# A two-layer decoder trunk: the undilated values are turned by VectorE and DMA, and statistics change row order by VectorE copies instead of fold matmuls

## The chip, the cores and the metric

The kernel runs on one core of a Trainium2 chip. The metric is the device time of one execution in microseconds, the median of three runs. Everything is float32; a product is made of three matmuls of rounded parts (high by high, low by high, high by low).

## The reference

The program computes a two-layer causal decoder for 512 tokens of width 1024. Layer 0 mixes tokens by a mixture of three dilated window attentions, layer 1 by differential attention; after each mixer come a squared-ReLU MLP and a gated input embedding. Only layer 0's mixer is touched by the change. Cut to what matters:

```python
# h: (1, 512, 1024); 16 heads of 64; groups (window, dilation) = (128,1), (512,4), (2048,16)
qkv = (h @ w_qkv).reshape(B, T, 3, 3, 16, 64)
for g in range(3):
    # query t attends to t, t-d, ..., t-window, with a bias by distance
    logits = q @ k.T * 64**-0.5 + bias ; lse = logsumexp(logits)
    out[g] = exp(logits - lse) @ v
alpha = softmax(stack(lse), axis=0)      # weight of each group, per position and head
o = sum(alpha * out) @ w_o
```

## The kernel before, in words

Tokens are in two row orders. The projections have them by residue mod 4 (all tokens with t mod 4 = 0, then 1, and so on): group 1 (dilation 4) has its rows in that order, and group 2 (dilation 16) uses the same tiles with a mask. The undilated group 0 needs its rows by position. So the statistics of group 0 (minimum and sum per row, `near_stat`) and those of groups 1 and 2 (`far_stat`) belong to differently ordered rows, and to merge the softmaxes they must be carried from one order to the other and back (`near_share`).

The first mixer runs in nine steps (`a_steps`): step s projects for pair s of heads and attends for pair s-1. Step 0 only projects, step 8 (the drain) only attends. Each step has nine slots; slot i has one projection unit of 24 matmuls of 512 columns on the tensor engine. In odd steps the first four slots are one large product for the values of groups 1 and 2 in four token tiles (`values_unit`, slots 0 to 3), evacuated by VectorE in slot 3 (L1423). The values of group 0 are projected in slot 0 of even and slot 4 of odd steps, and turned one slot later (`A_TURN_V`).

All orders are written out by hand. Each engine walks the slots, and within a slot the statements of its own `sub_a`:

- VectorE: masked logits and minimum (slots 0 and 1), the low part of the next unit's weights (`next_lo`, L1236), the merge of the statistics (slot 2), scaling of the four groups of probabilities (`scale_a`, L1324; slots 2, 3, 4, 5), a turn of each within 32x32 blocks (L1350; `blocks`), and at the slot's end the evacuation of the unit (L1436, L1423).
- GpSimd: when a group's blocks are ready, 16 DMAs put the blocks in their places (L902), 64 a step. Blocks and DMAs together transpose the probabilities.
- Tensor engine: scores (slots 0 and 1), the first fold in slot 2 (L1892), the second in slot 4 (L1901), the turn of the values in slot 1 or 5 (L1778), and at the end of slot 8 the value products of the four groups in the order 2, 3, 0, 1 (L1850), each of which waits until its 16 DMAs have landed.

A fold carries statistics between the row orders. VectorE spreads them against a pattern (`quarter`, L1356 and L1391), four small matmuls with `fold` sum rows 32 apart, and VectorE copies the result back from PSUM (L1365, L1397).

A unit waits for the evacuation of the units before it (L1716):

```python
wait(te, evac_done, u - (3 if is_first_up(u) else 2 if is_third(u) else 1))
```

For unit 4 of an odd step this means that the first three of the four evacuations (L1423) of the values' product are through.

Of the kernel before, what the change touches and what calls it, by code (L numbers as in the profile page):

```python
# [35 lines left out]
ALU = mybir.AluOpType  # L36
ACT = mybir.ActivationFunctionType

P = 128
# [3 lines left out]
NT = T // P  # L43
# [33 lines left out]
DRAIN_SPREAD, DRAIN_MERGE, DRAIN_NEAR = 3, 4, 6  # L77
# [171 lines left out]
def build(nc, x, p, rel_bias, a_w_qkv, a_w_o, b_w_qkv, b_w_o, lq1, lk1, lq2, lk2, subln, norm_mix,  # L249
          norm_mlp, w_ff1, w_ff2, norm_ple, w_gate, w_proj, final_norm, selector, out):  # L250
    ctx = ExitStack()
    with ctx:
# [61 lines left out]
        fold = sb("fold", [P, SUB])  # L314
        quarter = sb("quarter", [P, NT])
# [11 lines left out]
        spread_stat = merge[:, 0:64].rearrange("p (a r) -> p a r", r=NT)  # L327
        spread_share = merge[:, 64:96].rearrange("p (a b) -> p a b", b=NT)
# [29 lines left out]
        far_in = logits[:, 0:4 * NT]  # L358
# [43 lines left out]
        def near_in(has_proj):  # L402

            return (turned if has_proj else attn)[:, 0:2 * NT]

# [20 lines left out]
        def merge_slots(has_proj):  # L426

            return (A_SPREAD, A_MERGE, A_NEAR) if has_proj else (DRAIN_SPREAD, DRAIN_MERGE, DRAIN_NEAR)
# [133 lines left out]
        quarter_ready = sem("quarter_ready")  # L562
        fold_ready = sem("fold_ready")
# [29 lines left out]
        qk_ready = sem("qk_ready")  # L593
        vt_ps = sem("vt_ps")
# [6 lines left out]
        spread_stat_ready = sem("spread_stat_ready")  # L601
        far_ps = sem("far_ps")
# [3 lines left out]
        spread_share_ready = sem("spread_share_ready")  # L606
        near_ps = sem("near_ps")
# [245 lines left out]
        def _(pool):  # L853
# [7 lines left out]
            pool.memset(quarter[:, :], 0.0).then_inc(quarter_ready, 1)  # L861
            pool.wait_ge(quarter_ready, 1)
            for r in range(NT):
                pool.memset(quarter[r * SUB:(r + 1) * SUB, r:r + 1], 1.0).then_inc(quarter_ready, 1)
            pool.wait_ge(const_ready, 5)
            pool.wait_ge(quarter_ready, 1 + NT)
            pool.tensor_tensor(fold[:, :], ident[:, 0:SUB], ident[:, SUB:2 * SUB], ALU.add
                               ).then_inc(fold_ready, 1)
            for r in range(2, NT):
                pool.wait_ge(fold_ready, r - 1)  # L870
                pool.tensor_tensor(fold[:, :], fold[:, :], ident[:, r * SUB:(r + 1) * SUB], ALU.add
                                   ).then_inc(fold_ready, 1)

            pool.wait_ge(fold_ready, NT - 1)
# [23 lines left out]
            for n in range(A_ITEMS * (A_PAIRS - 1)):  # L898
                ph = A_TURN_ORDER[n % A_ITEMS]
                pool.wait_ge(blocks_ready, n + 1)  # L900
                for i, j in itertools.product(range(NT), range(NT)):
                    pool.dma_start(turned_order(probs[ph][j * SUB:(j + 1) * SUB, :])[:, i, :],  # L902
                                   turned_order(blocks[i * SUB:(i + 1) * SUB, ph, :])[:, j, :]
                                   ).then_inc(probs_landed[ph], 16)
# [10 lines left out]
        def _(sc):  # L915
# [96 lines left out]
            def sub_a(s, par, i, has_proj, has_attn):  # L1012
# [16 lines left out]
                _, merge_at, _ = merge_slots(has_proj)  # L1029
# [14 lines left out]
                if has_proj and i == A_TURN_V[par]:  # L1044

                    wait(sc, vt_ps, s + 1)
                    sc.activation(a_buf(par, 0, V), misc[:, :], ACT.Copy).then_inc(v_ready, 1)
# [90 lines left out]
            def sub_b(s, par, i, has_proj, has_scores, has_prev, has_norm):  # L1138
# [22 lines left out]
                if has_scores and i == 0:  # L1161
                    wait(sc, vt_ps, s + A_PAIRS)
                    sc.activation(b_buf(1 - par, V), misc[:, :], ACT.Copy).then_inc(v_ready, 1)
# [65 lines left out]
        def _(ve):  # L1229
# [63 lines left out]
            def start_statistics():  # L1293

                ve.wait_ge(quarter_ready, 1 + NT)
# [30 lines left out]

            def merged(s, n):
# [843 lines left out]
```

## Time and profile before

| | |
|---|---|
| time, median of 3 runs | 1594.29 us (1594.04 to 1595.57) |
| time of the profiled execution | 1594.29 us |
| its span | 1592.4 us |
| tensor engine busy | 1576.4 us, 99% |
| VectorE busy | 919.3 us, 58% |
| ScalarE busy | 590.9 us, 37% |
| GpSimd busy | 286.4 us, 18% |
| tensor engine's granted clock | 0.998 of 2.4 GHz |

The span is what lies between the first and the last instruction of the profiled execution; the time has about 2 us around it. Matmuls overlap: the busy time of one (0.39 us for 512 columns) is longer than the distance to the next start, so costs are read from starts. The steps of the first mixer are at about 68 to 124 us (step 1), then some 58 us each: step 4, an even one, is at 241 to 299 us, step 5, an odd one, at 299 to 357 us.

### The profile page before, as it was taken

To read this page: it belongs to the slowest core of one execution; us is meant where nothing else is said; L and a number is where in the kernel's file an instruction comes from. 1 tells how busy PE (TensorE), PEld (TensorE's weight loads), DVE (VectorE), ACT (ScalarE), POOL (GpSimd) and SP (SyncE) were. 2 spreads that over 40 slices of the span, in tenths; PEclk is the share of its full clock that TensorE was granted. 3 is DMA by queue.
4 is the path that set the end of the run, shared out by engine and by line. 5 is a ranking of instruction groups with operands and counts; after the bars stand their busy time and mean duration, and the time that the engine had idled before them with its cause. 6 is when DMAs were issued, how large, how long until landed. Compare 5 with 4: busy or idle time off the path is not lost.

```text
span 1592.4 us, 22054 instructions
## 1 busy us (share of the span) xinstructions
PE 1576.4 (99%) x8034; PEld 1296.5 (81%) x8034; DVE 919.3 (58%) x1585; ACT 590.9 (37%) x1064; POOL 286.4 (18%) x516
## 2 busy tenths in 40 slices
PE   9999999999999999999999999999999999999998
PEld 7888888888888788888888878888878888888886
DVE  5466466457456844536355766777685363545565
ACT  5324314324324522213123446676552131222344
POOL 2072473474470200000001110000020000000111
PEclk9999999999999999999999999999999999999999
DMA  6565464465443233333333332332233333333341
GB/s 166 151 166 145 141 171 129 140 166 133 120 126 112 79 104 88 100 92 97 100 92 99 99 118 69 106 92 72 73 93 98 90 104 94 92 103 92 93 116 70
DMA packets 314909, 174.84 MB, mean 110 GB/s; under 512 B 38713, under 2 KB 302450, under 8 KB 314850
## 3 DMA queue, kind: packets, MB, share of 16 engines
q1 hardware_dynamic: 300112, 158.61, 35.5%
q0 software_dynamic: 14480, 15.42, 3.5%
q8 instruction: 36, 0.59, 0.2%
q14 instruction: 23, 0.19, 0.0%
q10 hardware_dynamic: 258, 0.04, 0.0%
HBM read 157.11 MB, written 10.60 MB: 105 GB/s over the span
## 4 chain that ended last, share of the span: by engine, by line
PE 89%; POOL 5%; DMA 2%; DVE 1%; ACT 1%; SPq 1%; issue 0%; POOLq 0%; ACTq 0%; DVEq 0%
PE unit_out L1702 24%; PE unit_out L1704 24%; PE unit_out L1703 24%; POOL probs L902 4%; POOL sumsq L910 1%; PE attn L1850 1%; DMA w_raw<-in_a_w_qkv_dram 1%; PE attn L2098 1%; PE turned L1778 1%; PE unit_out L1869 1%; PE unit_out L1870 1%; PE unit_out L1871 1%; PE logits L1702 1%; PE misc L1778 1%; PE misc L1702 1%; PE misc L1704 1%
## 5 line engine op out<-in xcount | busy, mean ns | idle before, releaser
L1702 PE MATMUL unit_out<-act_hi,w_hi 128*128 128x512 f32 x1849 | 725.9, 393 | 1.6 <-DVE act_lo L1251 1.1
L1704 PE MATMUL unit_out<-act_hi,w_lo 128*128 128x512 f32 x1849 | 718.6, 389 | 0.0
L1703 PE MATMUL unit_out<-act_lo,w_hi 128*128 128x512 f32 x1849 | 718.0, 388 | 0.0
L928 ACT ACTIVATE w_hi<-w_raw 128x1024 fp32r<-128x1024 f32 (+3 forms) x256 | 270.9, 1058 | 464.2 <-PE unit_out L1704 368.3
L1702 PEld LDWEIGHTS unit_out<-act_hi,w_hi 128*128 128x128 f32 x1849 | 347.1, 188 | 77.3 <-DVE w_lo L1236 3.0
L1704 PEld LDWEIGHTS unit_out<-act_hi,w_lo 128*128 128x128 f32 x1849 | 347.1, 188 | 72.6
L1703 PEld LDWEIGHTS unit_out<-act_lo,w_hi 128*128 128x128 f32 x1849 | 347.4, 188 | 69.4 <-issue 0.2
L1236 DVE TENSOR_TENSOR w_lo<-w_raw,w_hi 128x1024 fp32r<-128x1024 f32 (+3 forms) x256 | 319.5, 1248 | 102.0 <-ACT w_hi L928 102.0
L902 POOL DMA_DIRECT2D probs<-blocks x448 | 220.3, 501 | 229.7 <-DVE blocks L1350 201.0
L910 POOL TENSOR_TENSOR sumsq<-sumsq,square 128x512 f32<-128x512 f32 x41 | 57.8, 1410 | 1053.6 <-ACT square L956 1051.8
L1098 ACT ACTIVATE act_hi<-hidden 128x512 fp32r<-128x512 f32 x64 | 40.5, 633 | 243.4 <-DVE hidden L1500 243.4
L1497 DVE TENSOR_TENSOR scaled<-unit_out,rstd 128x512 f32<-128x512 f32 x62 | 42.8, 690 | 67.8 <-PE unit_out L1704 67.7
L1315 DVE TENSOR_TENSOR h_a<-h_a,unit_out 128x512 f32<-128x512 f32 x39 | 26.8, 687 | 90.0 <-PE unit_out L1704 90.0
L1315 DVE TENSOR_TENSOR heads<-heads,unit_out 128x512 f32<-128x512 f32 x40 | 27.5, 686 | 84.2 <-PE unit_out L1704 84.2
L1037 ACT ACTIVATE probs<-probs,w_raw 128x256 f32<-128x256 f32 (+1 forms) x128 | 61.7, 484 | 28.2 <-DVE w_raw L1340 28.2
L1503 DVE TENSOR_TENSOR act_lo<-hidden,act_hi 128x512 fp32r<-128x512 f32 x64 | 44.3, 692 | 44.7 <-ACT act_hi L1098 44.7
L1500 DVE SCALAR_TENSOR_TENSOR hidden<-scaled 128x512 f32<-128x512 f32 x64 | 44.3, 692 | 2.2
L1581 DVE CUSTOM_DVE_ANT_0 probs<-logits,bias 128x512 f32<-128x512 f32 (+3 forms) x64 | 28.2, 487 | 26.0 <-PE logits L1704 26.0
L1154 ACT ACTIVATE probs<-probs,low 128x512 f32<-128x512 f32 (+3 forms) x64 | 35.4, 554 | 7.5 <-DVE low L1581 7.5
L1413 DVE TENSOR_TENSOR act_lo<-attn,act_hi 128x512 f32 (+1 forms) x8 | 5.5, 690 | 52.1 <-ACT act_hi L1051 52.1
L943 ACT ACTIVATE act_hi<-heads,gains 128x512 fp32r<-128x512 f32 x24 | 17.3, 722 | 49.1 <-DVE heads L1315 25.6
L1324 DVE TENSOR_SCALAR probs<-probs,w_raw 128x256 f32<-128x256 f32 (+1 forms) x128 | 35.4, 341 | 0.3
(296 smaller groups left out, 1384.2 us busy)
## 6 DMA issues: line engine op xcount, KB each, us to landing
w_raw<-in_w_ff_dram SPq DMA_DIRECT2D x128, 512.0 KB, 4.0
w_raw<-in_a_w_qkv_dram SPq DMA_DIRECT2D x56, 512.0 KB, 4.3
probs<-blocks POOLq DMA_DIRECT2D x448, 32.0 KB, 2.5
w_raw<-in_b_w_qkv_dram SPq DMA_DIRECT2D x24, 512.0 KB, 5.0
w_raw<-in_a_w_qkv_dram SPq DMA_DIRECT2D x32, 256.0 KB, 3.1
w_raw<-in_w_ple_gate_dram SPq DMA_DIRECT2D x16, 512.0 KB, 3.9
bias_tiles_b<-bias_vectors SPq DMA_DIRECT2D x16, 256.0 KB, 4.4
bias<-bias_tiles_b SPq DMA_DIRECT2D x8, 512.0 KB, 3.8
```

The lines of the kernel that those rows point to most:

```text
L902: pool.dma_start(turned_order(probs[ph][j * SUB:(j + 1) * SUB, :])[:, i, :], turned_order(blocks[i * SUB:(i + 1) * SUB, ph, :])[:, j, :]). ...
L910: pool.tensor_tensor(sumsq[:, :], sumsq[:, :], square[n % 2][:, :], ALU.add).then_inc(sumsq_done, 1)
L928: sc.activation(weights_of(u)[0][:, 0:width, :], w_raw[par][:, 0:width, :], ACT.Copy).then_inc(hi_done, 1)
L1037: e = sc.activation(probs[ph][:, cols], probs[ph][:, cols], ACT.Exp, bias=low_col, scale=-1.0, accum_out=sum_col)
L1236: ve.tensor_tensor(lo[:, 0:width, :], w_raw[par][:, 0:width, :], hi[:, 0:width, :], ALU.subtract).then_inc(lo_done, 1)
L1315: ve.tensor_tensor(h[:, n, :], h[:, n, :], unit_out[u.const % 2][:, :], ALU.add).then_inc(evac_done, 1)
L1497: ve.tensor_tensor(scaled[:, :], bank_of(u)[:, :], rstd[:, :], ALU.mult).then_inc(evac_done, 1)
L1500: ve.scalar_tensor_tensor(hidden[:, :], scaled[:, :], 0.0, scaled[:, :], ALU.max, ALU.mult).then_inc(hid_ready, 1)
L1503: ve.tensor_tensor(MID[layer][1][:, n, :], hidden[:, :], MID[layer][0][:, n, :], ALU.subtract).then_inc(hid_done, 1)
L1702: te.matmul(bank, w_k[0], hi, start=start, stop=False)
L1703: te.matmul(bank, w_k[0], lo, start=False, stop=False)
L1704: return te.matmul(bank, w_k[1], hi, start=False, stop=stop)
```

## The change

Four things are edited, all in the first mixer.

1. The four matmuls per pair that turn group 0's values, and ScalarE's copy of the result, are gone. VectorE turns them within 32x32 blocks into `probs_t`, and GpSimd puts the blocks in place by 16 DMAs per pair on a semaphore of their own. In even steps these DMAs stand ahead of the probabilities' 64 in GpSimd's order, in odd steps behind them. VectorE waits for the landing of the previous pair's values before it writes `probs_t` again.
2. Both folds are gone, with `quarter`, `fold` and the spreading. Instead 16 copies of 32 rows each carry the statistics, first from `near_stat` to `far_stat` (slot 2), later from `share` to `near_share` (slot 4).
3. The blocks of each group of probabilities are turned in the slot of their scaling, right behind it, and ahead of the slot's evacuation; before, one slot later and behind the evacuation.
4. The tensor engine waits for the values' landing before the third of its value products. In layer 1 only the counts of the semaphore `v_ready` change.

```diff
-A_SPREAD, A_MERGE, A_NEAR = 1, 2, 4
+A_MERGE, A_NEAR = 2, 4
 A_SCALES = {2: (2,), 3: (3,), 4: (0,), 5: (1,)}
+A_BLOCKS = A_SCALES
-A_BLOCKS = {3: (2,), 4: (3,), 5: (0,), 6: (1,)}
...
 # GpSimd
+            def spread_values(pair):
+
+                pool.wait_ge(values_blocks, pair + 1)
+                to = a_buf(pair % 2, 0, V).rearrange("p (a i q) -> p a i q", a=NT, i=NT)
+                for i, j in itertools.product(range(NT), range(NT)):
+                    pool.dma_start(to[j * SUB:(j + 1) * SUB, :, i, :],
+                                   probs_t[i * SUB:(i + 1) * SUB, j * P:(j + 1) * P].rearrange(
+                                       "p (a q) -> p a q", a=NT)).then_inc(values_landed, 16)
+
+            for step in range(A_PAIRS):
+                if step % 2 == 0:
+                    spread_values(step)
+                for n, ph in enumerate(A_TURN_ORDER) if step else ():
+                    pool.wait_ge(blocks_ready, A_ITEMS * (step - 1) + n + 1)
+                    spread(probs[ph], blocks[:, ph, :], probs_landed[ph])
+                if step % 2:
+                    spread_values(step)
...
 # VectorE, slot 2
-                    wait(ve, far_ps, s)
-                    ve.tensor_copy(far_stat[:, :, 0, :], far_in[:, :].rearrange(
-                        "p (a b) -> p a b", a=2)).then_inc(merge_step, 1)
+                    wait(ve, exp_done, (s - 1).times(A_ITEMS) + 2)
+                    far, near = (x.rearrange("p a (j b) -> p a j b", b=NT) for x in
+                                 (far_stat[:, :, 0, :], near_stat[:, :, :]))
+                    for b, r in itertools.product(range(NT), range(NT)):
+                        last = ve.tensor_copy(far[rows_of(b), :, :, r], near[rows_of(r), :, :, b])
+                    last.then_inc(merge_step, 1)
...
 # VectorE, slot 4
-                    wait(ve, near_ps, s)
-                    ve.tensor_copy(near_share[:, :], near_in(has_proj)).then_inc(near_share_ready, 1)
+                    near, far = (x.rearrange("p (j b) -> p j b", b=NT) for x in (near_share[:, :], share[:, 0, :]))
+                    for b, r in itertools.product(range(NT), range(NT)):
+                        last = ve.tensor_copy(near[rows_of(r), :, b], far[rows_of(b), :, r])
+                    last.then_inc(near_share_ready, 1)
                     wait(ve, near_share_ready, s)
                 if has_attn:
                     for ph in scales_at(has_proj, i):
                         scale_a(s, ph)
+                    for ph in blocks_at(has_proj, i):
+                        wait(ve, probs_ready, (s - 1).times(A_ITEMS) + (A_TURN_ORDER.index(ph) + 1))
+                        to_blocks(blocks[:, ph, :], probs[ph][:, :]).then_inc(blocks_ready, 1)
+                if has_proj and i == A_TURN_V[par]:
+                    wait(ve, evac_done, u)
+                    wait(ve, values_landed, s.times(16 * NT * NT))
+                    to_blocks(probs_t[:, :], a_v_t(i - 1)).then_inc(values_blocks, 1)
...
 # tensor engine
-                if has_proj and i == A_TURN_V[par]:
-                    wait(te, evac_done, u)
-                    wait(te, v_ready, s)
-                    turn(misc, [(a * P, a_v_t(i - 1)[:, a * P:(a + 1) * P])
-                                for a in range(NT)]).then_inc(vt_ps, 1)
                 if has_attn and i == A_UNITS - 1:
                     for n, ph in enumerate(A_TURN_ORDER):
+                        if ph == 0:
+                            wait(te, values_landed, s.times(16 * NT * NT))
                         if has_proj:
                             wait(te, probs_landed[ph], s.times(16 * NT * NT))
```

How this moves instructions is shown at three places. First VectorE in an odd step, from the turn of the first block to the end of slot 3 (before: one row further); `heads` are the four evacuations of the values' product, `blocks` the turned probabilities. Before:

```order
L1350 STREAM_TRANSPOSE blocks<-probs 128x8x4x32
L196 REGISTER_ALU
L1236 TENSOR_TENSOR w_lo<-w_raw,w_hi 128x1024
L1324 TENSOR_SCALAR probs<-probs,w_raw 128x256 x4
L196 ISA
L1423 TENSOR_SCALAR heads<-unit_out,start_scale 128x2x2x128
L196 REGISTER_ALU
L1423 TENSOR_SCALAR heads<-misc,start_scale 128x2x2x128
L196 REGISTER_ALU
L1423 TENSOR_SCALAR heads<-unit_out,start_scale 128x2x2x128
L1423 TENSOR_SCALAR heads<-attn,start_scale 128x2x2x128
L1350 STREAM_TRANSPOSE blocks<-probs 128x8x4x32
```

After:

```order
L1319 STREAM_TRANSPOSE blocks<-probs 128x8x4x32
L196 REGISTER_ALU
L1227 TENSOR_TENSOR w_lo<-w_raw,w_hi 128x1024
L1314 TENSOR_SCALAR probs<-probs,w_raw 128x256 x4
L1319 STREAM_TRANSPOSE blocks<-probs 128x8x4x32
L196 ISA
L1412 TENSOR_SCALAR heads<-unit_out,start_scale 128x2x2x128
L196 REGISTER_ALU
L1412 TENSOR_SCALAR heads<-misc,start_scale 128x2x2x128
L196 REGISTER_ALU
L1412 TENSOR_SCALAR heads<-unit_out,start_scale 128x2x2x128
L1412 TENSOR_SCALAR heads<-attn,start_scale 128x2x2x128
```

The turn of the second block, which stood after the fourth evacuation in slot 4, now stands ahead of the first one in slot 3.

Second VectorE in an even step, from the weight split of slot 1 to the end of the merge's first part in slot 2. Before:

```order
L1236 TENSOR_TENSOR w_lo<-w_raw,w_hi 128x1024
L1436 TENSOR_TENSOR hidden<-unit_out,rstd_q 128x4x4x32
L196 REGISTER_ALU
L1365 COPY w_raw<-logits 128x2x8
L196 REGISTER_ALU
L1368 TENSOR_TENSOR w_raw<-w_raw 128x8
L196 REGISTER_ALU
L1372 TENSOR_TENSOR w_raw<-w_raw 128x16
L196 REGISTER_ALU
L1236 TENSOR_TENSOR w_lo<-w_raw,w_hi 128x1024
```

After:

```order
L1227 TENSOR_TENSOR w_lo<-w_raw,w_hi 128x1024
L196 REGISTER_ALU
L1319 STREAM_TRANSPOSE probs_t<-scaled 128x4x4x32
L1425 TENSOR_TENSOR hidden<-unit_out,rstd_q 128x4x4x32
L1349 COPY w_raw<-w_raw 32x2x2 x16
L196 REGISTER_ALU
L1352 TENSOR_TENSOR w_raw<-w_raw 128x8
L196 REGISTER_ALU
L1356 TENSOR_TENSOR w_raw<-w_raw 128x16
L196 REGISTER_ALU
L1227 TENSOR_TENSOR w_lo<-w_raw,w_hi 128x1024
```

The turn of the values (`probs_t<-scaled`) is added in slot 1, and 16 copies of 32 rows stand where one copy from PSUM stood.

Third GpSimd's whole list of DMAs. Before:

```order
L892 CAST table<-probs 32x16
L895 DMA qk_hi<-selector_dram 96x1824
L896 DMA qk_hi<-selector_dram 1x16x114
L902 DMA probs<-blocks 32x256 x448
L910 TENSOR_TENSOR sumsq<-sumsq,square 128x512 x41
```

After:

```order
L873 DMA qk_hi<-selector_dram 96x1824
L874 DMA qk_hi<-selector_dram 1x16x114
L888 DMA heads<-probs_t 32x4x32 x16
L879 DMA probs<-blocks 32x256 x64
L888 DMA heads<-probs_t 32x4x32 x32
L879 DMA probs<-blocks 32x256 x128
L888 DMA heads<-probs_t 32x4x32 x32
L879 DMA probs<-blocks 32x256 x128
L888 DMA heads<-probs_t 32x4x32 x32
L879 DMA probs<-blocks 32x256 x128
L888 DMA heads<-probs_t 32x4x32 x16
```

The 16 DMAs of the first pair's values come first. Where x32 stands, 16 belong to the values of an odd step, behind its probabilities, and 16 to the next even step, ahead of its probabilities. The probabilities' transfers (32 rows of 256 elements) are 448 as before; the values' have 32 rows of 4 pieces of 32 elements.

## Rows read from the trace of the kernel before

**Rows 1.** The page's first part: busy us, share of the span, instructions.

```profile
PE 1576.4 (99%) x8034; PEld 1296.5 (81%) x8034; DVE 919.3 (58%) x1585; ACT 590.9 (37%) x1064; POOL 286.4 (18%) x516
```

**Rows 2.** PE's waits, 60 to 540 us: us in total, times, longest.

```profile
PE attn L1850 <- DMA probs<-blocks: 1.4, 2, 1.0
```

**Rows 3.** Timeline of PE, step 5 (odd): start us, us, engine, what.

```profile
325.23 0.39 PE L1871 MATMUL attn<-w_hi,act_lo 128*128 128x512 f32 x1
325.55 0.25 PE L1901 MATMUL turned<-w_raw,fold 128*32 128x8 f32 x8
...
327.67 0.39 PE L1704 MATMUL unit_out<-act_hi,w_lo 128*128 128x512 f32 x1
...
336.51 0.39 PE L1704 MATMUL unit_out<-act_hi,w_lo 128*128 128x512 f32 x1
336.75 0.60 PE L1778 MATMUL misc<-ident,scaled 128*128 128x128 f32 x4
...
339.95 0.39 PE L1702 MATMUL unit_out<-act_hi,w_hi 128*128 128x512 f32 x1
```

**Rows 4.** Timeline of PE, step 4 (even).

```profile
255.53 0.39 PE L1704 MATMUL unit_out<-act_hi,w_lo 128*128 128x512 f32 x1
255.77 0.60 PE L1778 MATMUL misc<-ident,scaled 128*128 128x128 f32 x4
256.29 0.26 PE L1892 MATMUL logits<-w_raw,fold 128*32 128x16 f32 x8
...
259.58 0.39 PE L1703 MATMUL unit_out<-act_lo,w_hi 128*128 128x512 f32 x1
```

**Rows 5.** Timeline of DVE, step 5, slot 3 and the start of slot 4.

```profile
322.45 1.15 DVE L1324 TENSOR_SCALAR probs<-probs,w_raw 128x256 f32<-128x256 f32 x4
323.53 0.74 DVE L1423 TENSOR_SCALAR heads<-unit_out,start_scale 128x512 f32<-128x512 f32 x1
...
324.85 0.73 DVE L1423 TENSOR_SCALAR heads<-unit_out,start_scale 128x512 f32<-128x512 f32 x1
...
326.33 1.23 DVE L1350 STREAM_TRANSPOSE blocks<-probs 128x1024 f32<-128x1024 f32 x1
```

**Rows 6.** Timeline of POOL, steps 4 and 5; in brackets the idle time before.

```profile
264.41 7.97 POOL L902 DMA_DIRECT2D probs<-blocks  x16 [27.07 <-DVE blocks L1350]
273.34 23.57 POOL L902 DMA_DIRECT2D probs<-blocks  x48 [0.97 <-issue]
...
337.07 15.62 POOL L902 DMA_DIRECT2D probs<-blocks  x32 [0.99 <-issue]
```

**Rows 7.** Line L902 alone: durations in ns, min/median/max.

```profile
L902 POOL DMA_DIRECT2D probs<-blocks x448: 496/496/631, 87.3 to 466.7; - x150
...
DMA to landing us min/median/max: 1.6/2.5/5.3
```

**Rows 8.** POOL's instructions on the tile qk_hi, the same columns.

```profile
L895 POOL DMA_DIRECT2D qk_hi<-selector_dram x1: 721/721/721, 15.9 to 15.9; - x1
L896 POOL DMA_DIRECT2D qk_hi<-selector_dram x1: 524/524/524, 16.6 to 16.6; - x1
```

**Rows 9.** Timeline of DVE, step 4, slots 1 to 3.

```profile
252.41 1.22 DVE L1236 TENSOR_TENSOR w_lo<-w_raw,w_hi 128x1024 fp32r<-128x1024 f32 x1
...
259.96 0.19 DVE L1391 TENSOR_TENSOR w_raw<-w_raw,quarter 128x32 f32<-128x32 f32 x1
260.07 1.13 DVE L1324 TENSOR_SCALAR probs<-probs,w_raw 128x256 f32<-128x256 f32 x4
...
262.88 1.23 DVE L1350 STREAM_TRANSPOSE blocks<-probs 128x1024 f32<-128x1024 f32 x1
```

**Rows 10.** Timeline of PE, the value products of steps 4 and 5.

```profile
295.21 2.62 PE L1850 MATMUL attn<-probs,heads 128*64 128x128 f32 x44
298.32 1.09 PE L1850 MATMUL attn<-probs,heads 128*64 128x128 f32 x16 [0.48 <-DMA probs<-blocks]
...
353.64 3.50 PE L1850 MATMUL attn<-probs,heads 128*64 128x128 f32 x60
```

More of the change, by code:

```diff
@@ L896, in _, with spread @@
             pool.dma_start(sel_sb[PIECES:PIECES + 1, :], selector[PIECES:PIECES + 1, :]).then_inc(s_sel, 16)
[L898 to L900 removed]
+            def spread(to, blocks_of, landed):
                 for i, j in itertools.product(range(NT), range(NT)):
[L902 to L904 removed]
+                    pool.dma_start(turned_order(to[j * SUB:(j + 1) * SUB, :])[:, i, :],
+                                   turned_order(blocks_of[i * SUB:(i + 1) * SUB, :])[:, j, :]
+                                   ).then_inc(landed, 16)
+            def spread_values(pair):
[13 more added lines that the diff above has]
+                    spread_values(step)
             for norm in range(1, 7):
@@ L1446, in sub_a @@
                         ve.tensor_tensor_reduce(
-                            out=probs_t[:, 0:E], in0=lam_in[:, 2 * n, :], in1=lam_in[:, 2 * n + 1, :],
+                            out=blocks[:, 1, 0:E], in0=lam_in[:, 2 * n, :], in1=lam_in[:, 2 * n + 1, :],
                             scale=1.0, scalar=0.0, op0=ALU.mult, op1=ALU.add,
@@ L1887, in sub_a @@
                     scores_a(par, ph).then_inc(scores_ready, 1)
-                if has_attn and i == merge_at:
-                    wait(te, spread_stat_ready, s)
-                    for b in range(NT):
-                        last = te.matmul(
-                            far_in[b * SUB:(b + 1) * SUB, :].rearrange("p (a r) -> p a r", r=NT),
-                            fold[:, :],
-                            spread_stat[:, :, :].rearrange("p (a b) r -> p a b r", b=NT)[:, :, b, :],
-                            start=True, stop=True)
-                    last.then_inc(far_ps, 1)
-                if has_attn and i == near_at:
-                    wait(te, spread_share_ready, s)
-                    for r in range(NT):
-                        last = te.matmul(
-                            near_in(has_proj)[r * SUB:(r + 1) * SUB, :].rearrange("p (j b) -> p j b", b=NT),
-                            fold[:, :],
-                            spread_share[:, :, :].rearrange("p (j r) b -> p j r b", r=NT)[:, :, r, :],
-                            start=True, stop=True)
-                    last.then_inc(near_ps, 1)
                 if has_attn:
@@ L2092, in sub_b @@
                     if i == 1:
-                        wait(te, v_ready, s + A_PAIRS)
+                        wait(te, v_ready, s)
                     wait(te, pt_a_ready, t - (ITEMS_A - A_ITEMS))
```

70 lines of the change are left out of this document (14 added, 56 removed).

## The prediction, made before the changed kernel was run

> **What bounds the kernel now.** The page's busy times come first: the tensor engine is busy for 99% of the span [rows 1], so the rule is that what it no longer executes is gained, and what keeps it waiting is lost. The list of what it waited for over the first mixer (60 to 540 us) is short: the only entry over 1 us is the wait of the value products for the DMAs of the turned probabilities, 1.4 us in two places [rows 2]. Next comes the timeline of one odd and one even step on the tensor engine [rows 3, 4], then what VectorE does around the same places [rows 5, 9], and last GpSimd's timeline [rows 6]. GpSimd issues 64 DMAs per step back to back, 0.496 us each [rows 7], some 31.5 us, and in the even step shown it ends just before the data is wanted. So there are two chains with almost no slack beside the full tensor engine, and the change touches both.
>
> **What is removed from the tensor engine.** The cost of an inserted group is read from starts. Undisturbed matmuls start every 0.2267 us (39 of them from 327.67 to 336.51) [rows 3]. Around the second fold of the odd step, nine intervals take 327.67 - 325.23 = 2.44 us instead of 2.04: 0.40 us. Around the four turns of the values, 13 intervals take 3.44 us instead of 2.95: 0.49 us. In the even step turns and first fold stand together, 14 intervals take 4.05 us instead of 3.17: 0.88 us [rows 4], so the first fold is 0.39. A step that both projects and attends saves 0.49 + 0.39 + 0.40 = 1.28 us; there are seven (four odd, three even): 9.0 us. The first step has only the turns, 0.5 us. The drain has only the folds, 0.8 us, but its scaling now stands behind 16 extra copies; I take 0.4, bounds 0 and 0.8. Sum: 9.9 us. ScalarE's copy of the turned values goes too; it is nowhere late, so nothing. The start loses some small GpSimd work that the rows do not show as waited for by the tensor engine: nothing.
>
> **What the odd step gives back (slot 3).** VectorE now turns the second block right behind its scaling, ahead of the four evacuations of the values' product. The tensor engine's unit 4 waits until the third of these is through (`evac_done`, count u-1, L1716). Before, the third starts at 324.85, takes about 0.73 like its neighbour (323.53 to 324.85 is two of them, 0.66 apart), ends at 325.58, and the engine is just done with the fold of 325.55: no slack [rows 3, 5]. After, the whole place is 0.39 us earlier (first fold gone), but the evacuation is 1.2 us later, the turn's 1.23 us [rows 5]: it ends at about 326.4. The engine would be ready at 325.23 + 0.23 - 0.39 = 325.07. Stall 1.3 to 1.4 us, taken 1.35, in each of four odd steps: 5.4 us. VectorE cannot take another order, and behind the stall the tensor engine has nothing else to do. Bounds: 0 (if I misread the count) and 1.6.
>
> **What the odd step's DMAs do.** Here the blocks still go before the values on GpSimd. It ends at 352.69 [rows 6]; the median landing is 2.5 us after issue [rows 7], so the last data is there about 354.7, and the last quarter of the value products starts at 353.64 + 3.50 - 1.09 = 356.05 [rows 10]. Since stall and saving cancel, this stays as it is: nothing.
>
> **What the even step gives back (GpSimd's queue).** The values' 16 DMAs stand ahead of the 64 of the probabilities. VectorE is through with slot 1's weight split at 252.41 + 1.16, then turns 512 columns, half of a block's 1.23 us, so done at 254.2; GpSimd started 0.3 us after such a turn before (262.88 + 1.23 to 264.41) [rows 6, 9], so it starts at 254.5. With p us per values DMA it reaches the probabilities at 254.5 + 16p. Their first block is ready a little before or after the old moment less 1.5 us: turning right behind scaling saves the evacuation ahead of it, the 16 copies cost 16 x 0.075 = 1.2 us (a 32-column operation is followed after 0.11 us, of which 0.033 are columns) [rows 9], and part of that hides in the wait for ScalarE. I put GpSimd's earliest start on the blocks at 262.8 to 264.1. After that 31.5 us and 2.0 us to the landing. The last quarter of the products was reached at 298.32 - 0.48 = 297.84 [rows 10], and will be at 296.56, 1.28 earlier. The wait is then W = 254.5 + 16p + 31.5 + 2.0 - 296.56 = 16p - 8.6, if p is over 0.52.
>
> **The price p.** No row shows a GpSimd DMA of this shape: 32 rows in 4 pieces of 128 bytes, 128 pieces, where the probabilities have 32 pieces of 1 KB. Below: 0.496, the probabilities' own price [rows 7]. Above: 96 rows cost 0.721 and a transfer of 16 pieces 0.524 [rows 8]; that is 2.5 ns a piece, and 128 pieces give 0.80; from 32 pieces at 0.496 to 96 at 0.721 they give 0.83. A third dimension may cost more, so I keep 1.0 as the end. I take 0.80, as the 96-row transfer is the nearest in pieces. W is 4.2 us. Three even steps wait 12.6 us, plus one pause of 0.97 between two runs of DMAs as at 272.38 [rows 6]: 13.6 us. The old waits of 1.4 us [rows 2] are inside this and come back. The Trainium skill (DMA: Bandwidth & Descriptors, on the anatomy of a GpSimd DMA) says: "You can emit a lot of descriptors before the incremental cost shows up". By it p is near 0.5 and the total is the first rival's; the 0.721 row speaks against it.
>
> **Other edits.** The near copies in slot 4 put 1.2 us before the third scaling; its block used to start after an evacuation and the probabilities' third run starts only 16 us after the first: hidden. VectorE waits for the previous values to land before it reuses `probs_t`; after an odd step GpSimd issues them for 12.8 us from about the step's end, landed some 15 us later, while VectorE asks 16 us into the step: hidden at 0.8, about 1.6 us late at p = 1.
>
> **The sum.** -9.9 (removed) + 5.4 (odd stalls) - 1.4 (old waits) + 13.6 (even waits) = +7.7 us. The profiled execution has a span of 1592.4 us and a time of 1594.29, which is also the median of the three runs, so 1594.3 + 7.7 = 1602.
>
> **The rivals.**
> A: GpSimd's price does not depend on the pieces. For it: 448 DMAs lie at 0.496, and one with half as many pieces costs no less. Against: 0.721. Then W is between -0.2 and 1.0, say 0.35, three times, and the pause: -9.9 + 5.4 - 1.4 + 2.0 = -3.9, so 1590.4. This is the case on the other side; it decides from p below 0.57 (W below 0.6). If the slot 3 stall fails as well, 1585.
> B: the price lies between, 0.57 to 0.69: 1591 to 1597.5, no change.
> C: p is 1.0, as the pieces are cut in three dimensions. W is 7.4, and the turn of the values waits 1.6 for the old ones: three times 9.0 and the pause, 28.0 us. Then -9.9 + 5.4 - 1.4 + 28.0 = +22, 1616.
> D: each small VectorE copy holds GpSimd back while it issues. Then 32 copies of 0.075 to 0.155 us add 2.4 to 5 us to each even step's queue, 7 to 15 us over three: 1609 to 1617. Against: GpSimd's DMAs stay at a median of 0.496 beside VectorE's scalings and turns [rows 7]; but none of those is a copy from SBUF to SBUF. The Trainium skill (SBUF — State Buffer, on the two separate sides) states this of fp32 copies: GpSimd "cannot write the descriptors" while they run. No row of this case shows it either way.
> E: no stall in slot 3, the price as forecast: 1596.6.
>
> **How the numbers follow.** About 0.2% (3.2 us) is what a measurement of this kernel can tell from no change. Forecast (p from 0.7 to 0.9) 0.42; A 0.22; B 0.14; C 0.09; D 0.07; E 0.06. Faster 0.23 (A and a little of E's kind), the same 0.19 (B and most of E), slower 0.58. The forecast's own range is 1598 to 1606 for p from 0.70 to 0.9. For 8 in 10 it must reach A and C: 1588 to 1617.
>
> **What would show it.** In the profile after: the groups of the folds and of the turned values are gone from the tensor engine and its busy time falls by about 10 us or a bit more, since modelled ends overlap; the first matmul of unit 4 in odd steps has an idle time of 1.3 us released by the `heads` evacuation; GpSimd's `heads<-probs_t` DMAs have a mean near 800 ns (this one number decides between forecast, A, B and C); the value products of steps 2, 4 and 6 wait about 4 us each for `probs<-blocks`; the probabilities' own DMAs stay at 496 ns (if not, D). The forecast is wrong if the mean is at or under 600 ns, or if the waits stand elsewhere than in these two places.

## The result: 3.8 us slower, half of what was forecast

| | before | after |
|---|---|---|
| time, median of 10 runs each | 1594.33 us | 1598.13 us |
| span of the profiled execution | 1592.4 us | 1595.9 us |

The ratio is 1.0024, with a 95% interval of 1.0016 to 1.0033. Slower was the likelier side, and the time lies in the range, but +3.8 us is not +7.7. The first part of the page after answers to [rows 1]:

```profile
PE 1570.9 (98%) x7874; PEld 1292.5 (81%) x7874; DVE 961.5 (60%) x1817; ACT 587.8 (37%) x1056; POOL 354.8 (22%) x636
```

160 small matmuls are gone and the busy time of the tensor engine is 5.5 us less, while the span has grown by 3.5. So it now waits for about 9 us more. Its list of waits, 60 to 540 us (us in total, times, longest), against the one entry of [rows 2]:

```profile
PE unit_out L1691 <- DVE heads L1412: 5.4, 4, 1.4
PE logits L1767 <- DVE probs L1314: 1.9, 1, 1.9
PE unit_out L1691 <- DVE w_lo L1227: 1.1, 3, 0.4
...
PE attn L1839 <- DMA probs<-blocks: 0.5, 1, 0.5
PE turned L1818 <- DVE w_raw L1335: 0.4, 2, 0.2
PE logits L1818 <- DVE w_raw L1335: 0.3, 1, 0.3
```

The first row is the forecast stall in slot 3, as idle time to the tenth. The forecast's largest term, 13.6 us of waits for the probabilities' DMAs, is the row with 0.5. The others were in no term. Why the DMAs are on time stands in GpSimd's rows (line alone: ns min/median/max; then its timeline in step 4), which answer to [rows 7] and [rows 6]:

```profile
L888 POOL DMA_DIRECT2D heads<-probs_t x128: 548/548/591, 28.2 to 475.7; - x128
```

```profile
254.76 8.65 POOL L888 DMA_DIRECT2D heads<-probs_t  x16 [8.79 <-DVE probs_t L1319]
264.86 31.54 POOL L879 DMA_DIRECT2D probs<-blocks  x64 [1.44 <-DVE blocks L1319]
```

A DMA of 128 pieces costs 0.548 us, not 0.80. The page's row of GpSimd's DMA queue (packets, MB, share), before and after, adds something:

```profile
q0 software_dynamic: 14480, 15.42, 3.5%
q0 software_dynamic: 18576, 17.52, 4.0%
```

The 128 new DMAs have 4096 packets, 32 each, and the 448 old ones have 32 each as well (14336 of the 14480). Counted in packets the two shapes are alike. How many descriptors (orders for a single piece) GpSimd writes for either, no row shows.

The 16 DMAs are through 1.44 us before the first block is there, so it is the block that GpSimd waits for. VectorE's timeline in step 4, slot 2, and in the last step, slot 6, answers to [rows 9]:

```profile
256.91 2.90 DVE L1349 COPY w_raw<-w_raw 32x4 f32<-32x4 f32 x16
...
508.69 2.76 DVE L1378 COPY w_raw<-w_raw 32x2 f32<-32x2 f32 x16
511.48 2.06 DVE L1314 TENSOR_SCALAR probs<-probs,w_raw 128x128 f32<-128x128 f32 x8
```

Sixteen copies take 2.8 to 2.9 us, 0.18 each, where the prediction had 0.075. In the last step the scaling stands right behind them, and the tensor engine waits for it (1.9 and 0.2 us). And at the start of steps 3 and 5, the two places where the loop over pairs of steps turns back, VectorE stops for something that no row of before has (here step 5):

```profile
303.19 0.29 DVE L1335 CUSTOM_DVE_ANT_0 probs<-logits,bias 128x128 f32<-128x128 f32 x1 [2.11 <-issue]
...
305.44 0.29 DVE L1335 CUSTOM_DVE_ANT_0 probs<-logits,bias 128x128 f32<-128x128 f32 x1 [1.95 <-issue]
```

"Issue" means idle time in which the engine waited for nothing that the profile shows. The scores are ready; the softmax of step 5 starts at 303.2 instead of 301.5.

**Where the 3.5 us come from.** Both kernels have the same 6273 matmuls of 512 columns, so the start of the n-th after less the start of the n-th before is a running balance. All its falls sum to -9.3 us: folds, turns and 0.9 us of DMA waits (the value products of steps 2 to 4 took 2.1 us over the undisturbed 3.50 each before, those of steps 2, 4 and 6 take 1.2 over it now). It rises at the start of unit 4 of odd steps by 4 x 1.20 (the stall, net of what the folds give there), in the drain by 2.40 + 0.34, in slot 6 of the even steps by 0.65, 0.65 and 0.56 (the two groups of copies make the `w_lo` split late), early in steps 3 and 5 by 0.73 and 0.93 (the late softmax), at the start of step 7 by 0.19 (step 6's value products take 3.65 us and not the undisturbed 3.50), at 49.6 us by 0.80, and by 0.22 near 1165 us. That is 12.3 - 9.3 = +3.0; the other 0.5 of the span lies behind the last of these matmuls.

### The profile page after: what moved, and what is told of

Its sections match the earlier page's. It is cut to its first block, busy times and chain, and to the rows that moved or that the text cites. A ratio compares the mean times of both kernels' runs of the same rounds, so it can differ in the third digit from the quotient of the medians.

```text
span 1595.9 us, 22073 instructions
## 1 busy us (share of the span) xinstructions
PE 1570.9 (98%) x7874; PEld 1292.5 (81%) x7874; DVE 961.5 (60%) x1817; ACT 587.8 (37%) x1056; POOL 354.8 (22%) x636
## 4 chain that ended last, share of the span: by engine, by line
PE 85%; POOL 5%; DVE 5%; issue 2%; DMA 1%; ACT 1%; SPq 0%; DVEq 0%; POOLq 0%; ACTq 0%
PE unit_out L1691 24%; PE unit_out L1693 24%; PE unit_out L1692 24%; POOL probs L879 4%; POOL sumsq L905 1%; PE attn L1839 1%; PE attn L2061 1%; PE turned L1767 1%; DVE w_lo L1227 1%; DMA w_raw<-in_a_w_qkv_dram 1%; PE logits L1691 1%; DVE probs L1314 1%; PE unit_out L1856 1%; PE misc L1691 1%; PE misc L1693 1%
## 5 line engine op out<-in xcount | busy, mean ns | idle before, releaser
L888 POOL DMA_DIRECT2D heads<-probs_t x128 | 69.4, 551 | 40.5 <-DVE probs_t L1319 40.5
```

Of the source, the lines that this page charges most:

```text
L888: pool.dma_start(to[j * SUB:(j + 1) * SUB, :, i, :], probs_t[i * SUB:(i + 1) * SUB, j * P:(j + 1) * P].rearrange("p (a q) -> p a q", a=NT) ...
```

## Experiments

The change has three parts: values, blocks, copies. The first four runs take one back or make one alone.

**The blocks back in their old slots.**

```diff
-A_BLOCKS = A_SCALES
+A_BLOCKS = {3: (2,), 4: (3,), 5: (0,), 6: (1,)}
 # and the block's turn again ahead of the copies and of the split of the weights
```

> The changed kernel with the probabilities' blocks back in the slots and the place where they were turned before (one slot after the scaling, ahead of the copies and the weights' split). Theory after the two traces: the 5.4 us that TensorE waits in slot 3 of the four odd steps come from the block's place between scaling and eviction alone, so they go: 1598.1 - 5.4 = 1592.7 us (1591.5 to 1594.5), and TensorE's waits for GpSimd's DMAs stay under 1 us. Rival 1, the stall comes from the 16 copies of slot 2 that run late into slot 3: it stays, 1597 to 1598.5. Rival 2, the queue on GpSimd needs the earlier blocks: the product of the values waits for DMAs in even steps by a slot's delay, 1600 or more.

Measured: 1597.88 us against 1594.72 of before in the same session, ratio 1.0017 (1.0008 to 1.0026). The stall is gone, as the theory says, but the time is far over its range:

```profile
PE attn L1839 <- DMA probs<-blocks: 4.3, 4, 1.7
```

```profile
49.07 0.39 PE L1693 MATMUL unit_out<-act_hi,w_lo 128*128 128x512 f32 x1
51.78 0.76 PE L1691 MATMUL unit_out<-act_hi,w_hi 128*128 128x512 f32 x1 [2.32 <-DVE w_lo L1227]
52.33 0.63 PE L1692 MATMUL unit_out<-act_lo,w_hi 128*128 128x512 f32 x1
```

The first is rival 2, smaller than it was put: with copies on VectorE the later blocks make the products of four steps wait. The second was in no expectation: in the first step the tensor engine waits 2.32 us and then starts a matmul every 0.43 us instead of every 0.23. The second costs 3.7 us there, against 0.8 in the profiled execution of the changed kernel, so together with the products' waits it eats up what the stall gave back. Both belong to other parts of the change, as the next runs show.

**The blocks alone.**

```diff
 # on the kernel before
-A_BLOCKS = {3: (2,), 4: (3,), 5: (0,), 6: (1,)}
+A_BLOCKS = A_SCALES
 # and the block's turn right behind scale_a
```

> The kernel before with only the blocks moved right behind the scaling; folds and the turn of the values on TensorE stay. Theory: four waits of 1.35 us in slot 3 of the odd steps, less 1.4 us of waits for DMAs that the earlier blocks take away: 1594.3 + 5.4 - 1.4 = 1598.3 us (1597.5 to 1600). Rival 1, the stall needs the copies of slot 2: 1593 to 1594.5. Rival 2, the earlier block also makes later weight splits late: over 1600.

Measured: 1597.08 us, ratio 1.0015 (1.0006 to 1.0024).

```profile
PE unit_out L1702 <- DVE heads L1423: 4.9, 4, 1.3
```

The theory holds in kind, just under its range: the stall is the block's place alone. No wait for a DMA is left in the list, and every group of 60 value products takes the undisturbed 3.50 us; of before, three of them took 3.68, 4.20 and 4.68. In the balance the stall costs 4 x 1.25 us and the shorter products give back 2.1, not 1.4: that is most of the 1.2 us.

**The values alone.**

```diff
 # on the kernel before
-turn(misc, [(a * P, a_v_t(i - 1)[:, a * P:(a + 1) * P]) ...   # TensorE, copied back by ScalarE
+to_blocks(probs_t[:, :], a_v_t(i - 1)).then_inc(values_blocks, 1)   # VectorE
+... spread_values(step)                                            # GpSimd, 16 DMAs
```

> The kernel before with only the undilated values turned in blocks and by GpSimd's DMAs; folds and the old places of the probabilities' blocks stay. Theory: eight times four turns at 0.49 us go from TensorE, -3.9 us, and the 16 DMAs at 0.55 us fit ahead of the probabilities: 1590.4 us (1589.5 to 1592), waits for DMAs in all under 2 us. Rival, the recorded term (0.80 us for a DMA) or any queue on GpSimd: the products of steps 2, 4 and 6 wait 1 to 4 us each, 1593 to 1603. Rival 2, VectorE's block turn of the values itself delays an eviction: +0.5 us a step, 1594.

Measured: 1592.98 us, ratio 0.9984 (0.9975 to 0.9993), outside the theory's range, and from 1589.7 to 1595.4 over the runs, where before has 1593.8 to 1597.1. No term for the queue appears: the products wait 0.5 us in all. What the profiled execution lost is at 51.6 us again. Its windows (window, its length, busy us and instructions of PE, PEld, DVE, ACT and POOL, granted clock, DMA share, GB/s):

```profile
49.00:50.00 1.00, 0.51 (x3) 0.08 (x1) 0.00 (x0) 0.74 (x1) 0.00 (x0) 1.00 0.88 149
...
53.00:54.00 1.00, 1.00 (x4) 0.81 (x3) 0.30 (x1) 0.00 (x0) 0.00 (x0) 0.50 0.91 267
...
56.00:58.00 2.00, 2.00 (x10) 1.63 (x10) 0.00 (x0) 0.00 (x0) 0.00 (x0) 1.00 0.18 48
```

Behind the wait of 2.1 us the granted clock is 0.50, 1.2 GHz, until about 56 us. In the balance that place costs 3.4 us, 1.9 from the later start and 1.5 from the clock. The wait is for a split of weights, the split for a load. SyncE's rows in the same stretch, before and with the values:

```profile
31.32 2.63 SPq L745 DMA_DIRECT2D bias_tiles_a<-bias_vectors  x4
...
39.68 3.29 SPq L713 DMA_DIRECT2D w_raw<-in_a_w_qkv_dram  x2
```

```profile
31.41 3.96 SPq L747 DMA_DIRECT2D bias_tiles_a<-bias_vectors  x4
...
41.42 3.29 SPq L715 DMA_DIRECT2D w_raw<-in_a_w_qkv_dram  x2
```

GpSimd issues the first pair's 16 DMAs in just this stretch (28.7 to 37.4 us), four of SyncE's issues take 3.96 us instead of 2.63, and the weights are asked for 1.7 us later. In all five profiled kernels that issue them here those four take 3.8 to 4.2 us, and 2.63 in the others. But only two of the five lose some 3.5 us at this place: the changed kernel and two others wait 0.9 to 1.1 us, stay at 1.00 and lose 0.7 to 0.9.

**The copies alone.**

```diff
 # on the kernel before
-te.matmul(far_in[...], fold, spread_stat ...) x8;  te.matmul(near_in[...], fold, spread_share ...) x8
+for b, r in itertools.product(range(NT), range(NT)):
+    last = ve.tensor_copy(far[rows_of(b), :, :, r], near[rows_of(r), :, :, b])
 # and the same for the near shares; spread_stat and spread_share go
```

> The kernel before with only the folds replaced by 32 copies a step on VectorE (the folds' constants are still made). Theory: TensorE loses 0.39 + 0.40 us a step, -6.2 us over eight steps; VectorE's copies at 0.18 us each cost +2.4 us in the last step, 0.6 us in slot 6 of each even step (+1.9), about 0.6 us at the start of each odd step (+1.9) and 0.8 us around step 1: 1594.3 - 6.2 + 7.0 = 1595.1 us (1593.5 to 1597). Rival, copies priced at 0.075 us as in the prediction: nothing is late, 1588 to 1589.5.

Measured: 1600.17 us, ratio 1.0031 (1.0019 to 1.0044). The terms of the theory are there, but one was missing:

```profile
PE attn L1846 <- DMA probs<-blocks: 5.5, 5, 2.1
PE logits L1774 <- DVE probs L1328: 1.9, 1, 1.9
```

With the blocks in their old place the copies and pauses run into the products' DMAs. Twice the tensor engine also came back at half clock, behind the wait in step 4's products and behind the one in the drain. The window behind the first:

```profile
301.00:303.00 2.00, 2.00 (x17) 1.78 (x16) 1.29 (x2) 0.98 (x1) 0.00 (x0) 0.50 0.02 4
```

The two stretches cost 1.5 and 1.6 us by the starts. The changed kernel waits 1.9 us at the same place of the drain and stays at 1.00.

So the three parts alone give +5.4, +2.4 and -1.7 us, together 6.1 and not 3.8. Two things are in that gap. With the copies the earlier blocks take more away: 4.3 us of the products' waits with the blocks late and 0.5 with them early. And the profiles of the copies alone and of the values alone have 3.1 and 1.5 us of half clock in them; those of before and after have none in these steps. How much of the gap is which, the medians don't tell.

**Values, step 0 held back.**

```diff
 # on "the values alone"
 pool.wait_ge(values_blocks, pair + 1)
+if pair == 0:
+    pool.wait_ge(evac_done, 8)
```

> The kernel before with only the values turned in blocks (as in the run with the values alone), and GpSimd holds the 16 DMAs of step 0 until the seventh unit is evicted (65 us), after SyncE has issued the step's bias tiles. Theory: in step 0 those DMAs slowed SyncE's issues (four bias tiles 3.96 us instead of 2.63), so the weights of the unit at 49.6 us came 2 us late and TensorE, after a wait of 2.1 us, ran at half clock for 3.5 us; held back, both go, and all of the 8 x 0.49 us shows: 1593.0 - 3.4 = 1589.6 us (1589.0 to 1590.8). Rival 1, the late weights have another cause than the 16 DMAs: 1592.5 to 1593.5, wait at 49 us still there. Rival 2, the same harm moves to the later place: a wait near 70 us, 1591 to 1594.

Measured: 1590.62 us, ratio 0.9972 (0.9961 to 0.9983), and the spread of the runs is back to 2.4 us. The wait at 49 us is gone. So the DMAs of step 0 cause it; that it goes by way of SyncE's longer issues is what the rows suggest. What is left of the distance to 1589.6 is a wait of step 2's products. With the values alone it was 0.3 us; why it is longer here stays open:

```profile
PE attn L1876 <- DMA probs<-blocks: 1.5, 1, 1.5
```

**Copies that nobody needs.**

```diff
 # on the kernel before, behind the eviction of slot 7
+for n in range(32):
+    ve.tensor_copy(extra[:, 2 * n:2 * n + 2], ident[SUB:2 * SUB, 2 * n:2 * n + 2])
```

> The kernel before with 32 small copies (32 partitions x 2 elements) a step added on VectorE behind the eviction of slot 7, where nothing waits for VectorE for some microseconds; folds stay, nothing reads what they write. Theory: the pauses of VectorE for issue at the start of each odd step (two of 2 us, 7.9 us in all in the three kernels with copies, none in those without) come from the number of instructions in the loop's body (about 229 with 2 steps before, 286 after) and not from what the copies do, so they appear here too, with 12 more packets in an instruction queue, and the time grows by 1 to 3 us: 1596.5 us (1595.3 to 1598). Rival 1, the pauses need the copies at their place: none here, 1594.3 to 1595. Rival 2, the copies' 5.8 us of VectorE itself make the next weights late: over 1598.

Measured: 1600.10 us, ratio 1.0033 (1.0021 to 1.0045). The pauses appear although nothing reads the copies:

```profile
DVE probs L1341 <- issue: 8.4, 4, 2.3
```

The page's row of one instruction queue (packets, MB, share) has 11 packets more than before's 23:

```profile
q14 instruction: 34, 0.28, 0.1%
```

The time grew by 5.5 us and not 2.2, to where rival 2 had it, but not by its mechanism: the 32 copies take 2.40 us and not 5.8, and nothing on the tensor engine waits for a split of weights. The late softmax costs only 1.0 us of it. The products take 4.4 us longer than before (sum over their groups) because the last DMAs land later. In step 4 everything is 3.42 us later than before when the blocks come, GpSimd's end too (300.33 instead of 296.91), yet the last quarter starts 2.4 us behind that end and not 1.4. SyncE's weight load, which waits for VectorE's split behind the copies, comes at 297.69 instead of 292.23, 2 us later than the shift, into the last of GpSimd's transfers. That the one delays the other is argued, not shown. And 1.5 us are the clock again, behind the longest wait, in step 2. The same 16 products in step 2 and step 4, then a window behind the first:

```profile
182.69 1.43 PE L1854 MATMUL attn<-probs,heads 128*64 128x128 f32 x16 [2.02 <-DMA probs<-blocks]
...
302.71 1.09 PE L1854 MATMUL attn<-probs,heads 128*64 128x128 f32 x16 [1.45 <-DMA probs<-blocks]
```

```profile
184.00:186.00 2.00, 2.00 (x20) 1.96 (x20) 1.00 (x2) 1.65 (x2) 0.00 (x0) 0.50 0.00 0
```

**Eight idle copies a step.**

```diff
 # on the kernel before, behind the eviction of slot 7
-for n in range(32):
+for n in range(8):
```

> As the run with 32 idle copies a step, with 8 a step: VectorE's body of two steps grows from about 229 to 245 instructions instead of 293. Theory: the pauses for issue start with the length of the body, which with 245 still fits: no pause, 1594.6 us (1594.3 to 1595.4). Rival, each added instruction costs its share: pauses of a quarter and 1595.8 us (1595.5 to 1597).

Measured: 1595.40 us, ratio 1.0006 (0.9997 to 1.0016), no row with "issue" for the softmax, 24 packets in that queue. VectorE's rows from the softmax of step 3 to that of step 5, one turn of the loop over two steps, number 226 before, 242 here, 282 with the copies alone, 286 after and 290 with 32 idle copies. The pauses come with the last three and not with the first two: a limit somewhere between 242 and 282, and not a share for each instruction.

**What a small copy costs.**

```diff
 # on the kernel before, last full step, 16 copies in each slot
+slot 5: ve.tensor_copy(ex[0:SUB, b, :, r], idn[SUB:2 * SUB, b, :, r])
+slot 6: ve.tensor_copy(extra[rows r, 32 + 2 * b:34 + 2 * b], ident[rows b, 2 * r:2 * r + 2])
+slot 7: ve.tensor_copy(ex[rows r, 6, :, b], idn[rows b, 0, :, r])
```

> The kernel before with three groups of 16 small copies (32 partitions x 2 elements) on VectorE in slots 5, 6 and 7 of the last full step, each behind the eviction: one from fixed partitions to fixed partitions with a stride between elements, one with changing partitions and elements side by side, one with changing partitions and a stride as in the changed kernel. The 32 idle copies of the other run (fixed partitions, elements side by side) came 0.075 us apart, those of the changed kernel 0.18 us. Theory: it is the change of partitions from one copy to the next that costs: 0.075, 0.18 and 0.18 us. Rival 1, the stride: 0.18, 0.075, 0.18. Rival 2, reading what was just written or waits between engines: 0.075 in all three.

Measured: 1593.26 us, one execution.

```profile
452.31 1.21 DVE L1443 COPY extra<-ident 32x2 f32<-32x2 f32 x16
458.12 2.92 DVE L1445 COPY extra<-ident 32x2 f32<-32x2 f32 x16
463.56 2.85 DVE L1448 COPY extra<-ident 32x2 f32<-32x2 f32 x16
```

Copies that keep their partitions follow each other after 0.076 us, those whose output moves to other partitions each time (their input every fourth time) after 0.18; the stride is free. The theory holds: 0.075 was the right price of a kind of copy that the change does not have.

**The drain's near copies one slot earlier.**

```diff
-DRAIN_MERGE, DRAIN_NEAR = 4, 6
+DRAIN_MERGE, DRAIN_NEAR = 4, 5
```

> The changed kernel with the 16 near copies of the last step one slot earlier (slot 5 instead of 6). Theory: TensorE's wait of 1.9 us for the scaled probabilities in slot 6 and the 0.5 us around it go, since slot 5 has idle time on VectorE: 1598.1 - 2.3 = 1595.8 us (1595 to 1596.8). Rival, the copies are late wherever they stand (slot 5 has head 3's scaling, for which slot 6 waits too): 1597.5 to 1598.5.

Measured: 1597.60 us, ratio 1.0023 (1.0013 to 1.0032); the profiled execution has 1596.49. By the medians 0.5 us under the changed kernel, less than the runs can tell. The wait moved rather than went:

```profile
PE turned L1767 <- DVE probs L1314: 1.4, 1, 1.4
```

From slot 5 to the end of the drain the balance rises by 1.30 us now and by 2.16 in the changed kernel. Slot 5 has room for a part of the copies only, so both stories are half right.

**Eight more DMAs in the even steps.**

```diff
 if step % 2 == 0:
     spread_values(step)
+    # for steps 2, 4, 6: 8 more DMAs of the same shape, into a tile that nobody reads
```

> The changed kernel with 8 more DMAs of the same kind (32 rows of four pieces of 128 bytes) behind the 16 of the values in steps 2, 4 and 6, into a tile that nobody reads. By the prediction's own term, W = n x p - 8.6 us with p as measured (0.548 us) and n = 24: a wait of 4.5 us for the probabilities in each of the three steps, +13 us; by the trace of after, where the queue was free 1.44 us before the first block of step 4 came, 8 x 0.548 - 1.44 = 2.9 us each, +9 us. So 1606 to 1612 us, and more if TensorE comes back at half clock behind such waits. Rival, the queue of GpSimd is hidden and has room: 1598 to 1600.

Measured: 1607.77 us, ratio 1.0083 (1.0068 to 1.0098), 9.6 us over the changed kernel.

```profile
PE attn L1845 <- DMA probs<-blocks: 8.1, 3, 2.7
```

2.7 us a step, where 8 x 0.548 - 1.44 gives 2.9 and the prediction's formula, with the measured price, 4.5. So the form of that term was right (the queue has a little room and then every DMA counts), its constant was 1.8 us too pessimistic and its price was off by more. A window behind the wait of step 4 and one behind that of step 6:

```profile
304.00:306.00 2.00, 2.00 (x27) 1.77 (x26) 1.29 (x2) 1.61 (x2) 0.00 (x0) 1.00 0.01 4
...
423.00:425.00 2.00, 2.00 (x20) 1.84 (x18) 0.87 (x2) 1.54 (x2) 0.00 (x0) 0.50 0.00 0
```

All three waits are 2.7 us long and stand at the same place of their step, yet only the third was followed by half clock. It cost 3.0 us of the 10.1 in the balance. So the fit of +9 forecast and 9.6 measured is in part luck: without the clock it would be about 7.

**Values held, and the blocks early except in slot 3.**

```diff
 # on "values, step 0 held back"
+A_BLOCKS = A_SCALES
+# slots 2, 4, 5: the block right behind the scaling
+# slot 3: the block behind the evictions of the slot
```

> The kernel before with the values turned in blocks (step 0's DMAs held back) and the probabilities' blocks right behind the scaling, except that in slot 3 the block of head 3 stands behind the eviction. Folds stay on TensorE. Theory: the earlier blocks take away what TensorE still waits for DMAs in the products (2.0 us over eight steps with the values held, none in the run with the blocks alone), and with slot 3's eviction first its 4.9 us don't come: 1590.6 - 2.0 = 1588.6 us (1587.8 to 1589.8). Rival 1, the eviction isn't what slot 3 waits for, or another one takes its place: 1590 to 1594. Rival 2, with the block of head 3 late the queue is no further than before: 1590 to 1591.

Measured: 1589.13 us, ratio 0.9970 (0.9957 to 0.9982). All three predicted effects: no wait of unit 4, 0.2 us of waits for DMAs, no pause. VectorE in slot 3 of step 5, against [rows 5]:

```profile
317.96 1.16 DVE L1341 TENSOR_SCALAR probs<-probs,w_raw 128x256 f32<-128x256 f32 x4
319.04 0.74 DVE L1447 TENSOR_SCALAR heads<-unit_out,start_scale 128x512 f32<-128x512 f32 x1
...
321.17 0.75 DVE L1447 TENSOR_SCALAR heads<-attn,start_scale 128x512 f32<-128x512 f32 x1
321.83 1.23 DVE L1346 STREAM_TRANSPOSE blocks<-probs 128x1024 f32<-128x1024 f32 x1
```

**The second fold as copies on ScalarE.**

```diff
 # on the run above; the near fold's 8 matmuls go, in slot 3 on ScalarE:
+for b, r in itertools.product(range(NT), range(NT)):
+    e = sc.activation(near[r * SUB:(r + 1) * SUB, :, b], far[b * SUB:(b + 1) * SUB, :, r], ACT.Copy)
```

> As the run with held values and blocks, and the second fold (near shares, 8 matmuls a step) is replaced by 16 copies on ScalarE in slot 3, of 32 partitions x 2 elements each, one slot ahead of their reader; the first fold stays on TensorE. Theory: VectorE's instructions in the loop's body stay under what they were, so no pauses for issue; ScalarE has room (37% busy) and TensorE loses 0.40 us a step: 3.0 us under the run beside it, 1585.6 us (1584.8 to 1587.5). Rival, ScalarE's 16 copies (at 0.2 us each 3.2 us) hold up the split of the next unit's weights: 1588 to 1592, with waits of TensorE for w_lo in slots 4 or 5.

Measured: 1587.94 us, ratio 0.9962 (0.9948 to 0.9975), the fastest of all: 6.5 us under the kernel before. Its step over the run above is 1.2 us by the medians, whose intervals overlap, and 1.7 by the spans, instead of 3.0; the time lies between the theory's range and the rival's, and no wait for the split of weights is in the list. ScalarE's copies take 0.203 us each:

```profile
L1065 ACT ACTIVATE w_raw<-w_raw 32x2 f32<-32x2 f32 x128 | 26.0, 203 | 1.4
```

In the balance the second fold's 0.4 us are gained in each even step and in the drain. In the odd steps they are not: there the fold stood where the tensor engine must wait for the third eviction anyway (no slack, [rows 3, 5]); that this is the cause is argued. Step 1's products lose 0.6 us to a wait for DMAs that the run beside it has not.

## Why the prediction missed

- **Removed work, -9.9 us.** Right. The balance falls by 9.3 with 0.9 of old waits in it, and 0.4 or more per odd step is hidden in the rise at unit 4; the values alone, held back, bring 3.7 us in the balance, near the 8 x 0.49 = 3.9.
- **Slot 3 of the odd steps, +5.4 us.** Right in place and cause: 5.4 of idle time in the trace, 4.9 with the blocks alone, none with the block behind the eviction. Measured from starts, as the removed work was, it is 4 x 1.6 = 6.4: the nine intervals around it in step 5 take 3.65 us instead of 2.04. The sum put idle time beside a saving read from starts, and was 1.0 us short by it.
- **The old DMA waits, -1.4 us, and GpSimd's queue in even steps, +13.6 us.** This is the step that failed, by its price p: 0.548 us measured against 0.80 taken, for 0.5 us of listed waits (1.2 by the length of the products) instead of 13.6. I had scaled a 96-row transfer of long rows by its number of pieces; the same trace had 448 DMAs at one flat price, and they were nearer in all but that number. 128 pieces cost 0.052 us more than 32. The Trainium skill's sentence (DMA: Bandwidth & Descriptors, on the anatomy of a GpSimd DMA) that many descriptors can be emitted before the cost shows agrees with this price. The rows don't prove it, since both shapes have 32 packets in the profile. The constant of the term was off too: in step 4 the last quarter of the products is due at 297.5 us and not 296.56, and it starts 1.4 us behind GpSimd's end of 296.40, not 2.0. With p alone put right, the sum is rival A's, 1590.4, and that is wrong too.
- **The small copies, nothing.** The second failed step, and it hid the first. I took the spacing of 0.11 us that follows an operation on 128 partitions and priced 32 copies at 0.075; they change partitions each time and cost 0.18, so 5.7 us of VectorE a step and not 2.4. They add 2.7 us in the drain, where the prediction even booked 0.4 us of gain, and 1.9 us in slot 6 of three even steps.
- **In no term at all:** the pauses at the loop's turn (late softmax, 1.7 us in steps 3 and 5), and 0.8 us in the first step (3.4 and 3.7 in the profiles of the values alone and of the late blocks), where I had asked only who waits for the queue's data and not what else was issuing in that stretch.
- **Rival D** (copies hold GpSimd back) is refuted: in step 4 the 16 copies at 256.91 lie inside the run of 16 DMAs from 254.76, which takes 8.65 us, the same as with the values alone, beside no copies. The 64 behind them take 31.54 us, before 31.54 as well. The Trainium skill's rule (SBUF — State Buffer, on the two separate sides) is not borne out here for copies this small.
- **That the time lies in the range is luck.** The even steps' DMAs were booked some 13 us too dear. The stall (1.0), the copies (4.6), the pauses (1.7) and the first step with the rest (1.0) were booked too cheap or not at all, about 8 us, and these errors cancel in part.

## To carry to other kernels

Where the tensor engine is full, price a replacement on another engine by the place where its result or its successor is waited for, and price a small instruction by a row of the same kind: same partitions or not is worth more than a factor of two. Count instructions where a loop is long, and look at what the other queues issue in the stretch into which a transfer is moved. Then split a change into its parts: of these three, one was worth 4 us, one cost 2.4 us until it gave way in one slot and then brought 1.5, and one should not have been made on this engine. Last, add up in one measure, starts or idle time. And read the granted clock behind every longer wait before a difference is put down to the change: it decided 1.5 to 3 us in five of these profiles.

## What was unexpected of the hardware

- VectorE, 32 partitions x 2 elements: 0.076 us from copy to copy with fixed partitions, 0.18 us when the partitions of the input or of the output change each time. ScalarE needs 0.203 us for the latter.
- With a loop body of 282 or more VectorE rows the engine pauses twice for 2 us at each turn, and 11 to 13 packets more go through an instruction queue; with one of 242 it does not.
- A GpSimd DMA costs 0.496 us of GpSimd with 32 pieces and 0.548 with 128; both count as 32 packets. While GpSimd issued 16 of them, four of SyncE's issues took 3.96 us instead of 2.63.
- After a wait of 2.1 to 2.3 us, TensorE's granted clock was 0.50 (1.2 GHz) for some 3 us; after the 1.0 us wait at the same place in the changed kernel it stayed 1.00. The length of the wait doesn't settle it: of three waits of 2.7 us in one execution two were followed by 1.00 and one by 0.50, and of two of 1.9 us in the drain of two kernels one by each. What settles it stays open.
